# Weight splitting moved within the scalar engine's tile order, output units interleaved, squares summed by VectorE

## Chip, core and metric

The kernel is one launch on one core of a Trainium2 chip. The metric is device time in microseconds (us) of that core; lower is better. Engines: TensorE (PE, with its weight load PEld), VectorE (DVE), ScalarE (ACT), GpSimd (POOL), and SyncE (SP), which issues most of the DMA.

## What is computed

Two identical-shaped decoder layers over 520 tokens (512 new prompt positions and 8 sampled tokens), width 1024, everything in float32. Cut to what matters here, with `rms` an RMS norm with a gain:

```python
x = x + 0.5 * swiglu(rms(x, n_ffn1), w_ffn1_gate, w_ffn1_up, w_ffn1_down)    # hidden 2816
mix, v, new_buf, hT = hybrid_mix(rms(x, n_mix), ...)       # ends in concat(y_a, y_b) @ w_out
x = x + mix
x = x + 0.5 * swiglu(rms(x, n_ffn2), w_ffn2_gate, w_ffn2_up, w_ffn2_down)
gate = sigmoid(rms(x, n_ple) @ w_ple_gate)
x = x + gate * (p @ w_ple_proj)
```

`swiglu(x, wg, wu, wd) = (silu(x @ wg) * (x @ wu)) @ wd`. After the second layer comes a final RMS norm. `hybrid_mix` is a gated spatial mixer beside a linear recurrence; it matters here through its last product, `w_out`.

## The kernel before

**Layout.** x lies in SBUF as 8 tiles of 128 features by 520 tokens (`x[:, o, :]`). Each float32 operand of a product is split into a rounded high part and a remainder (`w_hi`, `w_lo`, `part_hi`, `part_lo`), and a product is the sum of three matmuls (hi·hi, hi·lo, lo·hi). A norm is not applied to x: its gain is put in when x is split, and the row factor `rstd_b` multiplies results. The weights are one stream of 512 KB units, loaded by SP into four `raw` buffers in turn; the load of unit n waits until the semaphore `wlo` says that unit n-4 has been used up. ACT makes the high part (`hi`), DVE the low part (`lo`).

**The feed-forward with seven products.** Three of the four feed-forwards (all but the first) go through `seven_ffn`: gate and up weights of one hidden tile (128 features), each cut in two halves along the 1024 inputs, against x cut in two feature halves and two token halves (A1, A2), are a 2 by 2 block product done with seven products `P1` to `P7` in place of eight, Strassen-Winograd fashion. Each product is twelve matmuls of 260 columns. It wants sums: of weight halves (`tau1` to `tau4`, DVE) and of x blocks (`sigma`, DVE: four operations for each k of 4, from x[k] and x[k+4]; `sigma_hi` on ACT and `sigma_lo` on DVE split them). A feed-forward has 22 hidden tiles in chunks of 8, 8 and 6; after each chunk come 8 down units (`down_part`).

**The order of work** is written out by hand for every engine, with semaphores. For tile t (g stands for the tile of a loop step) PE runs `P1(g+1) P7(g) P2(g+1) P4(g) P6(g+1) P5(g+1) P3(g)`. P1 and P2 read the gate weights themselves, split in slot t % 2 (`gate_cut`): ACT writes `w_hi` (L1024) and the negated weights into `w_lo` (L1025), then POOL adds the weights to that `w_lo` by an accumulating DMA from DRAM (`gate_low`, L539), which leaves the remainder. P6 and P5 read the split of tau1 and tau2: `hi12` on ACT (L1031), `lo12` on DVE (L1489). P7 and P4 read that of tau3 and tau4: `hi34` (L1036), `lo34` (L1494). P3 reads one half of the up weights, `hi_b` (L1041) and `lo_b` (L1499). P4(g) may start only when DVE has read P7's result out of the same PSUM bank (`c22`, L1544: it adds the copy `p5` that ACT made of P5 at L1111). ACT's row for the gate weights is `gate(t)`, called for tile g+3 in loop step g, ahead of `copy_p5(g+1)` and `hi12` of tile g+2.

**Entry into such a feed-forward.** Before it stand 8 units that finish x, one feature tile each: the output projection (L1842 adds to x), or in layer 0's last stage the PLE gate units (L1884). Behind each, ACT (`seven_prep`) copies x times gain to `part_hi` (L1004), keeps x21g (L1009) and squares x into `rs` (L1012); DVE makes `part_lo` (L1431) and, for units 4 to 7, the block sums (`sigma`, L1440 to L1448); POOL adds up the squares (L424, L427). `seven_ahead` prepares the weights of the first tiles. PE then runs `P1(0) P1(1) P2(0)`, `stat1` (the sum of squares over partitions), `P2(1) P6(0) P5(0) P7(0) P4(0)`; ACT takes the root of `stat1`'s result and DVE its reciprocal (`rstd`, L1382).

Of the kernel before, what the change touches and what calls it, by code (L numbers as in the profile page):

```python
# [77 lines left out]

Y_ORDER = (MT, MT + 1, 0, MT + 2, 1, MT + 3, 2, 3)
# [68 lines left out]
def trunk(nc, weights, x_in, p_in, vecs_in, ln_in, bs_in, ws_in, bd_in, sc_in, sh_in,  # L148
          y_out, st_out, v_out):
    ctx = ExitStack()  # L150
    with ctx:
# [94 lines left out]
        gate_neg = sem("gate_neg")  # L246
        gate_lo = [sem(f"gate_lo{b}") for b in range(2)]
# [217 lines left out]
        def _(pool):  # L465
# [89 lines left out]
            for l in range(DEPTH):  # L555
# [17 lines left out]
                sums_and_gates(4 * l + 2, l, 1)  # L573
                sums(4 * l + 3)
                if l + 1 < DEPTH:
                    sums_and_gates(4 * l + 4, l + 1, 0)
                else:
                    sums(4 * l + 4)
# [7 lines left out]
        def _(pe):  # L586
# [49 lines left out]
            def seven_ffn(l, which, u0, g0):  # L636
# [24 lines left out]
                for c, tiles in enumerate(FFN_CHUNKS):  # L661
                    first = c == 0

                    def P1(t):
                        if t < 2:
                            pe.wait_ge(evac, G - 1 + t)
                        else:
                            pe.wait_ge(c21_ev, S + t - 1)
                        pe.wait_ge(gate_lo[gate_slot(t)], 16 * ((S + t) // 2 + 1))
                        kw = (lambda k: pe.wait_ge(xlo, XT * stat + k + 1)) if first and t == 0 else None  # L670
                        product(X(G, t), *gate_w(t, 0), *a11, True, False, kw).then_inc(prod, 1)

                    def P2(t):
                        kw = (lambda k: pe.wait_ge(xlo, XT * stat + KH + k + 1)) if first and t == 0 else None
# [67 lines left out]
                    pe.wait_ge(dlo_s, 2 * (3 * (S // HT0) + c) + 1)  # L742
# [1280 lines left out]
```

## Time and profile before

| | |
|---|---|
| median of 3 runs | 1999.06 us (1995.28 to 2002.83) |
| the profiled execution's own time | 2009.22 us |
| its span, first to last instruction | 2007.4 us |
| PE busy | 1906.4 us, 95% |
| DVE / ACT / POOL busy | 1315.3 / 894.1 / 197.0 us |
| granted TensorE clock, mean | 0.984 of full |

A profile is one execution. PE is busy nearly all the time, so the time is what PE's matmuls take plus the stretches in which PE stands, plus what matmuls lose while the granted clock is low. In a timeline row, the brackets say how long the engine was idle before and who ended that.

### The profile page before, as it was taken

Reading aid. Unit: us, or ns where it says so; the run is one execution under the profiler, and the core shown is the slowest. Engines: PE = TensorE matmul, PEld = TensorE weight load, DVE = VectorE, ACT = ScalarE, POOL = GpSimd, SP = SyncE. Lnnn points to the kernel's source line nnn. Section 1 sums busy time; section 2 is a strip of 40 time slices with the busy share of each in tenths; the row PEclk is TensorE's granted clock in tenths of the full one; section 3 lists DMA queues with packets and bytes.
Section 4 is the critical chain, followed back from the end, with each engine's and each line's share of the span. In section 5 each row is a group of like instructions: output and inputs, shape, how many; then the busy total and the mean of one; then the engine's idle time right before and its main releaser. Section 6 shows DMA issues by size and latency. Waiting matters only on the chain.

```text
span 2007.4 us, 37482 instructions
## 1 busy us (share of the span) xinstructions
PE 1906.4 (95%) x15280; PEld 1872.2 (93%) x15280; DVE 1315.3 (66%) x1889; ACT 894.1 (45%) x1271; POOL 197.0 (10%) x247
## 2 busy tenths in 40 slices
PE   8999999999989999999889999999998999999997
PEld 7999999999989989999888989999998999999996
DVE  6444434578687577577877567577777775766775
ACT  5222312454455354354555354344544553534443
POOL 1000000130100000001200000013202000000012
PEclk9999999999989999999989999999999999999998
DMA  5232222322345354454245354462223444544431
GB/s 203 86 103 85 93 87 93 114 76 75 95 116 143 106 127 141 102 144 134 74 106 134 111 126 145 99 175 97 74 96 95 121 142 100 132 127 115 137 125 47
DMA packets 63690, 225.83 MB, mean 112 GB/s; under 512 B 7152, under 2 KB 9488, under 8 KB 63552
## 3 DMA queue, kind: packets, MB, share of 16 engines
q1 hardware_dynamic: 52576, 184.87, 27.5%
q0 software_dynamic: 10976, 38.98, 10.9%
q8 instruction: 103, 1.69, 0.3%
q14 instruction: 35, 0.29, 0.0%
HBM read 221.52 MB, written 2.31 MB: 111 GB/s over the span
## 4 chain that ended last, share of the span: by engine, by line
PE 65%; DVE 12%; DMA 9%; ACT 8%; issue 5%; POOL 0%; DVEq 0%; SPq 0%; ACTq 0%; POOLq 0%
PE main L596 32%; PE main L736 10%; PE main L632 9%; DMA raw<-weights_dram 8%; PE aux L632 4%; PE aux L736 4%; PE aux L888 2%; ACT w_hi L1031 2%; DVE w_lo L1370 2%; ACT w_lo L1025 2%; ACT w_hi L984 1%; ACT wx L1041 1%; DVE x L1622 1%; DVE tau L1478 1%; DVE tmp L1544 1%
## 5 line engine op out<-in xcount | busy, mean ns | idle before, releaser
L596 PE MATMUL main<-part_hi,w_hi 128*128 128x260 f32 x1888 | 382.4, 284 | 3.4 <-DVE tmp L1643 1.5
L596 PE MATMUL main<-part_hi,w_lo 128*128 128x260 f32 x1888 | 380.1, 283 | 0.0
L596 PE MATMUL main<-part_lo,w_hi 128*128 128x260 f32 x1888 | 379.3, 282 | 0.0
L1370 DVE TENSOR_TENSOR w_lo<-raw,w_hi 128x1024 fp32r<-128x1024 f32 (+1 forms) x194 | 245.8, 1269 | 86.5 <-ACT w_hi L984 82.6
L984 ACT ACTIVATE w_hi<-raw 128x1024 fp32r<-128x1024 f32 (+1 forms) x212 | 218.0, 1033 | 187.2 <-PE main L736 84.7
L632 PE MATMUL main<-part_hi,w_hi 128*128 128x260 f32 x792 | 235.9, 298 | 65.8 <-DVE tmp L1544 44.1
L596 PEld LDWEIGHTS main<-part_hi,w_hi 128*128 128x128 f32 x1888 | 291.6, 188 | 5.8 <-issue 3.4
L596 PEld LDWEIGHTS main<-part_hi,w_lo 128*128 128x128 f32 x1888 | 290.6, 188 | 0.0
L596 PEld LDWEIGHTS main<-part_lo,w_hi 128*128 128x128 f32 x1888 | 290.0, 188 | 0.0
L632 PE MATMUL main<-part_lo,w_hi 128*128 128x260 f32 x792 | 228.9, 289 | 0.0
L632 PE MATMUL main<-part_hi,w_lo 128*128 128x260 f32 x792 | 228.6, 289 | 0.0
L632 PEld LDWEIGHTS main<-part_hi,w_hi 128*128 128x128 f32 x792 | 153.4, 194 | 78.6 <-DVE tmp L1544 55.1
L632 PE MATMUL main<-sig,w_hi 128*128 128x260 f32 x1056 | 200.6, 287 | 0.0
L736 PE MATMUL main<-part_hi,w_hi 128*128 128x260 f32 x816 | 164.6, 283 | 3.0 <-DVE x L1622 3.0
L632 PEld LDWEIGHTS main<-sig,w_hi 128*128 128x128 f32 x1056 | 166.8, 193 | 0.0
L736 PE MATMUL main<-part_hi,w_lo 128*128 128x260 f32 x816 | 164.5, 283 | 0.0
L736 PE MATMUL main<-part_lo,w_hi 128*128 128x260 f32 x816 | 163.9, 282 | 0.0
L632 PEld LDWEIGHTS main<-part_lo,w_hi 128*128 128x128 f32 x792 | 154.5, 195 | 0.1
L632 PEld LDWEIGHTS main<-part_hi,w_lo 128*128 128x128 f32 x792 | 154.4, 195 | 0.0
L632 PE MATMUL main<-sig,w_lo 128*128 128x260 f32 x528 | 151.3, 287 | 0.0
L1036 ACT ACTIVATE w_hi<-tau 128x1024 fp32r<-128x1024 f32 x66 | 70.1, 1062 | 179.3 <-DVE tau L1484 157.0
L539 POOL DMA_DIRECT2D w_lo<-weights_dram x66 | 57.3, 869 | 899.5 <-ACT w_lo L1025 899.1
(253 smaller groups left out, 3665.0 us busy)
## 6 DMA issues: line engine op xcount, KB each, us to landing
raw<-weights_dram SPq DMA_DIRECT2D x344, 512.0 KB, 3.4
w_lo<-weights_dram POOLq DMA_DIRECT2D x66, 512.0 KB, 5.4
x<-x_in_dram SPq DMA_DIRECT2D x4, 520.0 KB, 7.1
y_out<-x SPq DMA_DIRECT2D x8, 260.0 KB, 2.7
mix<-p_in_dram POOLq DMA_DIRECT2D x2, 520.0 KB, 3.8
tau<-ln_dram POOLq DMA_DIRECT2D x2, 512.0 KB, 4.0
tau<-ws_dram POOLq DMA_DIRECT2D x2, 512.0 KB, 4.7
bs<-bs_dram POOLq DMA_DIRECT2D x2, 256.0 KB, 4.1
```

The costliest lines, as they stand in the source:

```text
L539: pool.dma_start(w_lo[:, gate_slot(t), :], weights[n, :, :], accum_op=ALU.add).then_inc(gate_lo[gate_slot(t)], 16)
L596: last = pe.matmul(ps[:, q, 0:HALF], ww[:, s, w], xx[:, k, q * HALF:(q + 1) * HALF], start=(a == 0 and b == 0), stop=(a == kts - 1 and b = ...
L632: last = pe.matmul(ps, ww[:, w], xx(k), start=(start and k == 0 and b == 0), stop=(stop and k == KH - 1 and b == 2), skip_group_check=True)
L736: last = pe.matmul(ps[:, q, 0:HALF], ww[:, j % SLOTS, w], xx[:, k, q * HALF:(q + 1) * HALF], start=(k == 0 and b == 0), stop=(k == tiles - ...
L888: last = pe.matmul(vbank[t] if t < NCH else vs, xx[:, k, c:c + P], ww[:, (U_V + u) % SLOTS, kk * WA:(kk + 1) * WA], start=(k == 0 and b == ...
L984: act.activation(w_hi[:, s, 0:c], raw[:, s, 0:c], ACT.Copy).then_inc(whi, 1)
L1025: act.activation(w_lo[:, gate_slot(t), :], raw[:, n % SLOTS, :], ACT.Copy, scale=-1.0).then_inc(gate_neg, 1)
L1031: act.activation(w_hi[:, 3, :], tau12, ACT.Copy).then_inc(whi, 2)
L1036: act.activation(w_hi[:, 2, :], tau34, ACT.Copy).then_inc(hi34_s, 1)
L1041: act.activation(wx_hi, raw_up(n, 1), ACT.Copy).then_inc(hib_s, 1)
L1370: dve.tensor_tensor(w_lo[:, s, 0:c], raw[:, s, 0:c], w_hi[:, s, 0:c], ALU.subtract).then_inc(wlo, 1)
L1478: dve.tensor_tensor(tau[:, 2 * HB:3 * HB], raw_up(n, 0), raw_up(n, 1), ALU.add)
```

## The change

- `gate_cut` writes `w_lo` first, then `w_hi`, with a semaphore of its own (`gate_hi`); P1 waits for both. In the tile loop ACT calls `gate(g + 2)` behind `hi_b(g)`, in place of `gate(g + 3)` behind `copy_u2(g + 1)`; the low part of down unit 1 is made by DVE in the last tile (`lo(d + 1, 1)`), not ahead of it.
- `ORDER` = (0, 4, 1, 5, 2, 6, 3, 7): output projection and PLE gate units come in this order (the weight stream too), so that x[k] and x[k+4] are finished one behind the other, and the block sums are made at every second unit, not at each of the last four. The regions for the split block sums (`SIG_HI`, `SIG_LO`) are placed anew, and the split of p moves from unit 2 to units 0 and 1.
- For the norms ahead of the seven-product feed-forwards DVE adds the squares (`add_square(dve, ...)`); POOL keeps the accumulating DMAs, and the sums of the other norms.
- `rstd` at the entry is moved ahead of `lo_b(0)`.

```diff
+ORDER = tuple(k for h in range(XT // 2) for k in (h, h + XT // 2))
...
-            def sums_and_gates(stat, l, which):
-
-                for o in range(1, XT):
-                    add_square(pool, stat, o)
-                    if o == XT - 3:
-                        gate_low(l, which, 0)
-                    if o == XT - 2:
-                        gate_low(l, which, 1)
-                for t in range(2, HT0):
+            def gates(l, which):
+
+                for t in range(HT0):
                     gate_low(l, which, t)
...
+                        pe.wait_ge(gate_hi, S + t + 1)
                         pe.wait_ge(gate_lo[gate_slot(t)], 16 * ((S + t) // 2 + 1))
-                        kw = (lambda k: pe.wait_ge(xlo, XT * stat + k + 1)) if first and t == 0 else None
+                        kw = (lambda k: pe.wait_ge(xlo, XT * stat + 2 * k + 1)) if first and t == 0 else None
...
             def gate_cut(n, t, T_):
 
                 act.wait_ge(raw_in[n % SLOTS], 16 * (n // SLOTS + 1))
-                act.activation(w_hi[:, gate_slot(t), :], raw[:, n % SLOTS, :], ACT.Copy)
                 act.activation(w_lo[:, gate_slot(t), :], raw[:, n % SLOTS, :], ACT.Copy,
                                scale=-1.0).then_inc(gate_neg, 1)
+                act.activation(w_hi[:, gate_slot(t), :], raw[:, n % SLOTS, :], ACT.Copy).then_inc(gate_hi, 1)
...
                     copy_u2(1)
-                    gate(3)
                     copy_p5(1)
                     hi12(n + 4, S + 2)
                     for g in range(1, tiles - 1):
                         act.wait_ge(unit, n + 2 * g)
                         hi_b(n + 2 * g, S + g)
+                        gate(g + 2)
                         copy_p1(g + 1)
                         h_hi(g - 1)
                         done(g, "P4")
                         hi34(n + 2 * g + 2, S + g + 1)
                         silu(g)
                         copy_u2(g + 1)
-                        gate(g + 3)
                         copy_p5(g + 1)
...
                     h_hi(t - 1)
+                    gate(t + 2)
                     silu(t)
...
-                    if KH <= o < XT - 1:
-                        sigma_hi(4 * l + 2, o - KH)
+                    if o % 2 and o < XT - 1:
+                        sigma_hi(4 * l + 2, o // 2)
...
                     lo12(n, S)
                     if first:
+                        add_square(dve, stat, XT - 1)
                         sigma_lo(stat, KH - 1)
+                        rstd(stat)
                     lo_b(n, S)
                     tau1(n + 2, S + 1)
                     tau2(n + 2, S + 1)
                     c11(0)
-                    if first:
-                        rstd(stat)
                     c11_r(0)
...
                             down_lo(0)
-                            down_lo(1)
                     t = tiles - 1
                     c12(t - 1)
-                    lo_b(n + 2 * t, S + t, 3)
+                    lo_b(n + 2 * t, S + t, 2)
                     c22(t)
                     hidden(t - 1)
                     h_lo(t - 1)
+                    lo(d + 1, 1)
                     c21(t)
...
+                    x_o = x[:, ORDER[o], :]
+                    dve.tensor_tensor(halves(x_o), pair(main[main_slot(G0 + G_OUT + o)]),
+                                      halves(x_o), ALU.add).then_inc(evac, 1)
+                    if o == 2:
+                        dve.wait_ge(p_v, l + 1)
+                    if o and o % 2 == 0:
+                        sigma_lo(4 * l + 2, o // 2 - 1)
+                    if o >= 2:
+                        add_square(dve, 4 * l + 2, o - 1)
                     seven_x_lo(4 * l + 2, o)
-                    if o >= KH:
-                        sigma(4 * l + 2, o - KH)
+                    if o % 2:
+                        sigma(4 * l + 2, o // 2)
```

How the instructions stand, in three places. First ACT in one step of the tile loop, before (L1024 and L1025 are the gate cut, L1111 `copy_p5`, L1031 `hi12`, L1041 `hi_b`):

```order
L1105 ACTIVATE mix<-main0 128x260
L1024 ACTIVATE w_hi<-raw 128x1024
L1025 ACTIVATE w_lo<-raw 128x1024
L1111 ACTIVATE mix<-aux0 128x260
L1031 ACTIVATE w_hi<-tau 128x1024
L1041 ACTIVATE wx<-raw 128x512
L1099 ACTIVATE mix<-main1 128x260
L1126 ACTIVATE part1_hi<-tmp 128x520
L1036 ACTIVATE w_hi<-tau 128x1024
```

and with the change (L1021 and L1023 are the gate cut, L1108 `copy_p5`, L1028 `hi12`, L1038 `hi_b`):

```order
L1102 ACTIVATE mix<-main0 128x260
L1108 ACTIVATE mix<-aux0 128x260
L1028 ACTIVATE w_hi<-tau 128x1024
L1038 ACTIVATE wx<-raw 128x512
L1021 ACTIVATE w_lo<-raw 128x1024
L1023 ACTIVATE w_hi<-raw 128x1024
L1096 ACTIVATE mix<-main1 128x260
L1123 ACTIVATE part1_hi<-tmp 128x520
L1033 ACTIVATE w_hi<-tau 128x1024
```

The gate cut has gone from ahead of `copy_p5` and `hi12` to behind `hi_b`, and its two copies have changed places.

Second, DVE behind output unit 6 of layer 0, from the addition to x up to the tau sum, before:

```order
L1842 TENSOR_TENSOR x<-main0,x 128x520
L1456 TENSOR_TENSOR sig<-tmp45,sig 128x780
L1458 TENSOR_TENSOR part0_lo<-tmp45,part0_hi 128x260
L1431 SCALAR_TENSOR_TENSOR part0_lo<-x,vecs,part0_hi 128x520
L1440 SCALAR_TENSOR_TENSOR tmp45<-x,vecs,tmp 128x260
L1442 SCALAR_TENSOR_TENSOR tmp45<-x,vecs,tmp 128x260
L1445 SCALAR_TENSOR_TENSOR tmp45<-x,ngain,tmp45 128x260
L1448 SCALAR_TENSOR_TENSOR tmp45<-x,ngain,tmp45 128x260
L1484 TENSOR_TENSOR tau<-tau,raw 128x512
```

and with the change (L429 is the addition of squares):

```order
L1841 TENSOR_TENSOR x<-main0,x 128x520
L1454 TENSOR_TENSOR sig<-tmp45,sig 128x780
L1456 TENSOR_TENSOR part0_lo<-tmp45,part0_hi 128x260
L429 TENSOR_TENSOR rs<-rs 128x520
L1429 SCALAR_TENSOR_TENSOR part0_lo<-x,vecs,part0_hi 128x260
L1482 TENSOR_TENSOR tau<-tau,raw 128x512
L1841 TENSOR_TENSOR x<-main1,x 128x520
L429 TENSOR_TENSOR rs<-rs 128x520
```

Unit 6 has lost its five-operation block (a full-width `part_lo` and four block sums) for one addition of squares and a half-width `part_lo`.

Third, DVE from the last weight split ahead of the feed-forward to the addition `c22` of its first tile, before:

```order
L1494 TENSOR_TENSOR w_lo<-tau,w_hi 128x1024
L1489 TENSOR_TENSOR w_lo<-tau,w_hi 128x1024
L1456 TENSOR_TENSOR sig<-tmp45,sig 128x780
L1458 TENSOR_TENSOR part0_lo<-tmp45,part0_hi 128x260
L1499 TENSOR_TENSOR wx<-raw,wx 128x512
L1466 TENSOR_TENSOR tau<-raw 128x512
L1472 TENSOR_TENSOR tau<-tau,raw 128x512
L1531 TENSOR_TENSOR tmp<-main0,mix 128x260
L1382 RECIPROCAL rstd_b<-rstd_b 128x520
L1535 TENSOR_TENSOR tmp<-tmp,rstd_b 128x260
L1544 TENSOR_TENSOR tmp<-main0,mix 128x260
```

and with the change:

```order
L1492 TENSOR_TENSOR w_lo<-tau,w_hi 128x1024
L1487 TENSOR_TENSOR w_lo<-tau,w_hi 128x1024
L429 TENSOR_TENSOR rs<-rs 128x520
L1454 TENSOR_TENSOR sig<-tmp45,sig 128x780
L1456 TENSOR_TENSOR part0_lo<-tmp45,part0_hi 128x260
L1379 RECIPROCAL rstd_b<-rstd_b 128x520
L1497 TENSOR_TENSOR wx<-raw,wx 128x512
L1464 TENSOR_TENSOR tau<-raw 128x512
L1470 TENSOR_TENSOR tau<-tau,raw 128x512
L1529 TENSOR_TENSOR tmp<-main0,mix 128x260
L1533 TENSOR_TENSOR tmp<-tmp,rstd_b 128x260
L1542 TENSOR_TENSOR tmp<-main0,mix 128x260
```

An addition of squares has come in ahead of the split of the last block sums, and the reciprocal stands ahead of `lo_b`, `tau1`, `tau2` and `c11`, no longer behind them.

## Rows read from the trace of the kernel before

**Rows 1.** First part of the page: busy us (share), instructions of each engine.
```profile
PE 1906.4 (95%) x15280; PEld 1872.2 (93%) x15280; DVE 1315.3 (66%) x1889; ACT 894.1 (45%) x1271; POOL 197.0 (10%) x247
```
**Rows 2.** Waits of PE: engine, line, releaser, us in total, times, longest.
```profile
PE main L632 <- DVE tmp L1544: 44.1, 47, 2.5
PE main L632 <- DMA w_lo<-weights_dram: 15.6, 3, 6.2
```
**Rows 3.** Waits of the other engines.
```profile
ACT w_hi L1024 <- DMA raw<-weights_dram: 93.2, 37, 4.3
...
DVE tau L1466 <- issue: 8.3, 8, 1.9
```
**Rows 4.** Timeline of ACT, DVE, PE, one loop step: start, us, row, [idle before].
```profile
724.70 1.06 ACT L1024 ACTIVATE w_hi<-raw 128x1024 fp32r<-128x1024 f32 x1 [2.62 <-DMA raw<-weights_dram]
...
726.87 1.05 ACT L1031 ACTIVATE w_hi<-tau 128x1024 fp32r<-128x1024 f32 x1
...
723.51 0.69 DVE L1472 TENSOR_TENSOR tau<-tau,raw 128x512 f32<-128x512 f32 x1
...
727.95 1.23 DVE L1489 TENSOR_TENSOR w_lo<-tau,w_hi 128x1024 fp32r<-128x1024 f32 x1 [2.26 <-ACT w_hi L1031]
729.10 0.42 DVE L1544 TENSOR_TENSOR tmp<-main,mix 128x260 f32<-128x260 f32 x1
...
729.57 0.38 PE L632 MATMUL main<-part_hi,w_hi 128*128 128x260 f32 x1 [0.81 <-DVE tmp L1544]
```
**Rows 5.** Timeline of PE, waits ahead of P4: two first tiles, one inner tile.
```profile
571.39 0.39 PE L632 MATMUL main<-part_hi,w_hi 128*128 128x260 f32 x1 [2.04 <-DVE tmp L1544]
...
606.03 0.39 PE L632 MATMUL main<-part_hi,w_hi 128*128 128x260 f32 x1 [2.15 <-DVE tmp L1544]
...
706.86 0.39 PE L632 MATMUL main<-part_hi,w_hi 128*128 128x260 f32 x1 [0.52 <-DVE tmp L1544]
```
**Rows 6.** Stretches of 25 us: length, busy (x) per engine, PEclk, DMA share, GB/s.
```profile
600.00:625.00 25.00, 22.86 (x178) 22.65 (x177) 19.62 (x32) 14.09 (x22) 1.71 (x2) 0.93 0.49 127
...
1050.00:1075.00 25.00, 22.54 (x177) 22.33 (x176) 17.93 (x29) 12.89 (x20) 1.73 (x2) 0.93 0.53 131
...
1725.00:1750.00 25.00, 22.68 (x186) 22.26 (x185) 19.01 (x33) 13.57 (x21) 1.75 (x2) 1.00 0.57 144
```
**Rows 7.** Landing of the accumulating DMAs (line L539), then of the raw loads (L445).
```profile
DMA to landing us min/median/max: 5.1/5.4/7.5
...
DMA to landing us min/median/max: 3.1/3.4/9.5
```
**Rows 8.** Timeline of PE at the three entries: P1 waits, and P4(0) of the third.
```profile
557.33 0.56 PE L632 MATMUL main<-part_hi,w_hi 128*128 128x260 f32 x1 [4.95 <-DMA w_lo<-weights_dram]
...
1000.28 0.56 PE L632 MATMUL main<-part_hi,w_hi 128*128 128x260 f32 x1 [5.17 <-DVE tmp L1387]
...
1553.51 0.56 PE L632 MATMUL main<-part_hi,w_hi 128*128 128x260 f32 x1 [6.15 <-DMA w_lo<-weights_dram]
...
1567.81 0.38 PE L632 MATMUL main<-part_hi,w_hi 128*128 128x260 f32 x1 [2.04 <-DVE tmp L1544]
```
**Rows 9.** Timeline of DVE, ACT and POOL at the first entry.
```profile
542.48 1.57 DVE L1440 SCALAR_TENSOR_TENSOR tmp<-x,vecs,tmp 128x260 f32<-128x260 f32 x1
543.97 0.48 DVE L1442 SCALAR_TENSOR_TENSOR tmp<-x,vecs,tmp 128x260 f32<-128x260 f32 x1
...
547.22 0.69 DVE L1842 TENSOR_TENSOR x<-main,x 128x520 f32<-128x520 f32 x1
...
567.15 3.39 DVE L1382 RECIPROCAL rstd_b<-rstd_b 128x520 f32<-128x520 f32 x1
...
549.51 1.05 ACT L1024 ACTIVATE w_hi<-raw 128x1024 fp32r<-128x1024 f32 x1
...
542.46 1.31 POOL L427 TENSOR_TENSOR rs<-rs 128x520 f32<-128x520 f32 x1 [4.74 <-ACT rs L1012]
...
551.81 0.88 POOL L539 DMA_DIRECT2D w_lo<-weights_dram  x1 [0.80 <-ACT w_lo L1025]
```

More of the change, by code:

```diff
@@ L246, in trunk @@
         gate_neg = sem("gate_neg")
+        gate_hi = sem("gate_hi")
         gate_lo = [sem(f"gate_lo{b}") for b in range(2)]
@@ L572, in _ @@
                 pool.dma_start(praw, p_in[l]).then_inc(p_s, 16)
-                sums_and_gates(4 * l + 2, l, 1)
+                gates(l, 1)
                 sums(4 * l + 3)
                 if l + 1 < DEPTH:
-                    sums_and_gates(4 * l + 4, l + 1, 0)
+                    gates(l + 1, 0)
                 else:
@@ L668, in P1 @@
                             pe.wait_ge(c21_ev, S + t - 1)
+                        pe.wait_ge(gate_hi, S + t + 1)
                         pe.wait_ge(gate_lo[gate_slot(t)], 16 * ((S + t) // 2 + 1))
-                        kw = (lambda k: pe.wait_ge(xlo, XT * stat + k + 1)) if first and t == 0 else None
+                        kw = (lambda k: pe.wait_ge(xlo, XT * stat + 2 * k + 1)) if first and t == 0 else None
                         product(X(G, t), *gate_w(t, 0), *a11, True, False, kw).then_inc(prod, 1)
                     def P2(t):
-                        kw = (lambda k: pe.wait_ge(xlo, XT * stat + KH + k + 1)) if first and t == 0 else None
+                        kw = (lambda k: pe.wait_ge(xlo, XT * stat + 2 * k + 2)) if first and t == 0 else None
                         product(Y(G, t), *gate_w(t, 1), *a12, True, True, kw).then_inc(prod, 1)
@@ L984, in hi, with prep @@
                 act.activation(w_hi[:, s, 0:c], raw[:, s, 0:c], ACT.Copy).then_inc(whi, 1)
-            def prep(stat, o):
-                n = stat * XT + o
+            def prep(stat, o, j=None):
+                j = o if j is None else j
+                n = stat * XT + j
                 if 0 < stat < 4 * DEPTH:
@@ L1307, in _ @@
                     seven_prep(4 * l + 2, o)
-                    if o == 2:
+                    if o == 0:
                         act.wait_ge(p_s, 16 * (l + 1))
@@ L1482, in tau4 @@
                 dve.wait_ge(t12, 2 * T_ + 2)
-                dve.wait_ge(gate_neg, T_ + 1)
+                dve.wait_ge(gate_hi, T_ + 1)
                 dve.tensor_tensor(tau[:, 3 * HB:4 * HB], tau[:, HB:2 * HB], raw_gate(n, 1), ALU.add).then_inc(wlo, 1)
@@ L1841, in _ @@
                     dve.wait_ge(unit, N + U_OUT + o + 1)
-                    dve.tensor_tensor(halves(x[:, o, :]), pair(main[main_slot(G0 + G_OUT + o)]),
-                                      halves(x[:, o, :]), ALU.add).then_inc(evac, 1)
-                    if o > KH:
-                        sigma_lo(4 * l + 2, o - KH - 1)
+                    x_o = x[:, ORDER[o], :]
[3 more added lines that the diff above has]
+                        dve.wait_ge(p_v, l + 1)
+                    if o and o % 2 == 0:
+                        sigma_lo(4 * l + 2, o // 2 - 1)
+                    if o >= 2:
+                        add_square(dve, 4 * l + 2, o - 1)
                     seven_x_lo(4 * l + 2, o)
-                    if o >= KH:
-                        sigma(4 * l + 2, o - KH)
-                    if o == 2:
+                    if o % 2:
+                        sigma(4 * l + 2, o // 2)
+                    if o == 1:
                         dve.wait_ge(p_a, l + 1)
@@ L1874, in _ @@
                         seven_x_lo(4 * l + 4, o - 1)
-                        if o > KH:
-                            sigma(4 * l + 4, o - 1 - KH)
+                        if o % 2 == 0:
+                            sigma(4 * l + 4, o // 2 - 1)
+                        if o >= 2:
+                            add_square(dve, 4 * l + 4, o - 1)
                     if o < (XT - 3 if l + 1 < DEPTH else XT - 1):
@@ L1881, in _ @@
                     dve.wait_ge(f_s, l * FS + HT0 + FS_MIX + HT0 + o + 1)
-                    dve.tensor_tensor(T(2), T(1), proj[:, o, :], ALU.mult).then_inc(x_tmp, 1)
+                    dve.tensor_tensor(T(2), T(1), proj[:, ORDER[o], :], ALU.mult).then_inc(x_tmp, 1)
                     dve.wait_ge(x_tmp, l * XT + o + 1)
-                    dve.tensor_tensor(x[:, o, :], x[:, o, :], T(2), ALU.add).then_inc(x_new, 1)
-                    if o > KH and l + 1 < DEPTH:
-                        sigma_lo(4 * l + 4, o - 1 - KH)
+                    dve.tensor_tensor(x[:, ORDER[o], :], x[:, ORDER[o], :], T(2), ALU.add).then_inc(x_new, 1)
+                    if o and o % 2 == 0 and l + 1 < DEPTH:
+                        sigma_lo(4 * l + 4, o // 2 - 1)
                 if l + 1 < DEPTH:
```

43 lines of the change are left out of this document (21 added, 22 removed).

## Prediction

> **What bounds the kernel now.** I read the page's busy shares first: PE is busy 95% of the span [rows 1], so matmuls set the time and only two things can be won: time in which PE stands, and time lost to a low clock. The change takes no matmul away. Then the waits of PE [rows 2]: 44.1 us in 47 waits end with DVE's `c22` (L1544), 15.6 us in 3 waits with an accumulating DMA into `w_lo`. Where the 47 stand is seen in the timeline of PE [rows 5, 8]: three are P4 of the very first tile of a seven-product feed-forward, 2.04 us each (571.39 and 1567.81 are two of them); six are P4 of the first tile of a later chunk, 0.52 us each (706.86 is one; there P4 follows P7 directly, so it must wait for `c22`, 0.42 us long). The other 38, 44.1 - 6.1 - 3.1 = **34.9 us**, are inner tiles, where P2 stands between P7 and P4 to cover `c22`, and yet PE waits 0.2 to 2.5 us.
>
> Why `c22` is late is read from one loop step of three engines [rows 4]. tau2 is done at 724.2, so `hi12` could be split. But ACT stands 2.62 us for a raw gate tile it needs only two tiles later, cuts it (two copies, some 1.9 us), copies p5, and starts `hi12` at 726.87. DVE, in its own fixed order, stands 2.26 us for it, does `lo12` (1.23) and then `c22` at 729.10; PE starts P4 at 729.57, 0.81 late. The wait of the whole kernel behind this is ACT's 93.2 us at L1024 for raw loads, 37 times [rows 3].
>
> **The change, part by part.** The sum is made against the profiled execution's 2009.2 us, which is 10 us above the median of 1999.06; gains are taken off the median unchanged.
>
> *1. Gate cut behind `hi_b`.* Let T be the end of P3 in the step shown: P4 at 729.57 less 0.81 less three products of twelve matmuls (1.43 us each) gives T = 724.5. With the change `hi12` waits for tau2 and p5 alone: start about 724.3, end 725.3 = T+0.9. DVE does `c12` and `hidden` until T+1.2, `lo12` until T+2.4, and is free before P7 ends at T+2.9; `c22` ends at T+3.4, P2 at T+4.3. The wait is gone with 0.9 us to spare. That margin covers the steps in which tau1 itself is late for its raw load, 8 times and at most 1.9 us [rows 3]: `hi12` moves by that, up to 1 us past the margin in the one worst. I take 2 us as what is left in 38 tiles: **33 us** gained, bounds 17 (half the waits stay) and 34.9.
>
> What is moved past what: the cut is now one tile ahead in place of two. It begins at T+1.4 behind `hi12` and `hi_b`, the `w_lo` copy ends T+2.4, POOL issues 0.3 later (at 551.81, where two copies begun at 549.51 end near 551.5 [rows 9]), and the DMA lands 5.4 us on [rows 7], at T+8.1. (The steps of T are the lengths in [rows 4], with 0.3 to 0.7 us for the short operations.) P1 of that tile stands at T+10.0 (seven products). So 1.9 us of slack; the slowest landing, 7.5 us [rows 7], comes at T+10.2. The second copy (`w_hi`, the new `gate_hi`) ends at T+3.4 and holds nobody: `tau4` of that tile comes a step later. The raw tile was asked for at `tau4` of the step before, T-4.9, and is there at T-1.5 by the median of 3.4 us [rows 7]. `copy_p1` goes back by 2 us to T+3.7, and P6 wants it at T+5.7. I cost all this at nothing; if the cover goes, it is P1 that waits.
>
> The Trainium skill (DMA: Bandwidth & Descriptors, "Anatomy of one DMA — SWDGE (gpsimd) path") gives a fit of 2.0 us plus bytes over 436 GB/s, which by the page would be an estimated 3.2 us for 512 KB. The row says 5.4 for this accumulating kind, and I use the row; by the page the slack would be 2 us more and each entry about 1 to 2 us quicker.
>
> *2. The clock.* A stretch with a wait of 2.15 us (606.03) shows 0.93 granted, so does the one with the longest inner wait; a stretch in which inner waits were at most 1.5 us shows 1.00 [rows 5, 6]. Between the two levels, 1.2 and 2.4 GHz, 0.93 over 25 us costs 25 x 0.07 = 1.75 us of full-clock work. Two such stretches, part of it lying in the wait itself: **3 us** (0 to 3.5).
>
> *3. The entries* (output projection into feed-forward, both layers; PLE gates into feed-forward, once). Let U be the end of the last unit: 557.33 - 4.95 - 1.43 = 550.95. Today the addition of unit 6 waits for DVE, busy with block sums, until 547.22, and ACT starts the second gate cut at 549.51; POOL issues at 551.81, and P1(1) starts at U+6.4, P4(0) at U+20.4 (571.39) [rows 5, 8, 9]. Two things in the rows slow DVE: the block sums of four units in a row, and POOL's additions of squares: the block-sum operation beside POOL's 542.46 row takes 1.57 us, its neighbour 0.48. With the change neither is there. DVE adds unit 6 at U-5.65, ACT begins the cut some 1.7 us later, the `w_lo` copy ends at U-2.9, issue U-2.6, landing **U+2.8**: P1(1) starts there, 3.6 us earlier. Now a new wait: `stat1` needs the sum of squares, whose last addition DVE makes behind `lo12`. P1(1) ends U+4.2, its copy and `hi12` U+5.65, `lo12` U+6.85, the addition (0.7) U+7.5, while PE has ended P2(0) at U+5.65: PE stands 1.9 us where it did not. `stat1` ends U+8.6, the root U+9.3, the reciprocal (3.39 [rows 9]) U+12.7, then `lo_b`, tau1, tau2, `c11` and its scaling (0.35 to 0.7 each) U+15.4, `c22` U+15.9. P4(0) at **U+15.9** where it was U+20.4: 4.5 us. In layer 1 P4(0) stands at 1567.81, with U = 1553.51 - 6.15 - 1.43 = 1545.93: U+21.9, so 6 us. POOL loses seven additions per entry (1.31 us each, off the path), DVE gains them at some 0.7 us each and gives that back by the lost slow operations.
>
> At the PLE entry every unit also costs DVE a scaling, a product and an addition to x. By the lengths above an even unit asks some 7.4 us of DVE and an odd one 4.2, beside 5.75 us of PE: DVE stays late, the second cut's DMA lands within a microsecond of where it does now, and P1(0) (5.17 us idle [rows 8]) moves back by up to 2.4. I take 0, bounds -2 and +2. Entries in all **10 us** (4 to 13).
>
> *4. Chunk ends.* `lo` of down unit 1 now stands in the last tile ahead of `c21`. ACT's silu of that tile ends some 0.1 us later than today; nine chunks: **-0.5 us** (-3 to 0). Interleaving, moved `sig` regions and the earlier split of p add no operation and are ahead of their readers: 0.
>
> Sum: 33 + 3 + 10 - 0.5 = 45.5, so the profiled execution would come at 1963.7 and the median at about **1953 us**.
>
> **Rivals.** *A, the wait stays in part.* `hi12` is freed from the gate cut, but DVE has only some 1.5 us idle per tile of 10; a raw load or `tau2` may be late each time once the step is 0.9 us shorter (tau1 waits already 8 times [rows 3]). Then half the inner waits stay: 17 + 1.5 + 5 = 23 us gained, 1976. *B, no change:* inner tiles are then held by tau1 in nearly every step and the entries lose at `stat1` what they win at P1(1): within 10 us of 1999. Against it: at 723.51 tau2 was in time and the waiting was all ACT's. *C, slower.* The accumulating DMA, with one tile of lead in place of two, is late for P1 in the 39 inner tiles that take their cut in the loop. It decides from a landing 1.9 us above the median; to eat the gain and 10 us more it must wait (45 + 10) / 39 = 1.4 us in each, a landing of 8.7 us where the slowest of 66 took 7.5 [rows 7]. That gives 2009. *D, everything comes:* no inner wait left, the clock at 1.00 through the entries too (their stretches lose several us more), 55 us: 1944.
>
> **Chances.** Forecast with its own spread (1946 to 1962) 0.60, D 0.14, A 0.18, B 0.04, C 0.04. The range takes in A and D: 1942 to 1976. About 0.5% (10 us) is what a measurement of this kernel can tell from no change. Faster by more than that: the forecast, A and D, 0.92; same 0.04; slower 0.04.
>
> **What would show it.** Step 1: PE's waits on `c22` fall from 44.1 us to about 10 (three first tiles of about 1.6, six of 0.52, a rest), ACT's 93.2 us wait for raw loads at the gate cut nearly vanishes, and new PE waits on the DMA at P1 of inner tiles stay few. Step 3: P1(1) about 2.8 us behind the last unit in the two output-projection entries, a new wait of about 2 us ahead of `stat1` that ends with DVE's addition of squares, block sums without a 1.5 us member. Wrong would be: `lo12` still waiting 2 us for `hi12`, PE waiting at P1 for the DMA in every tile, or a PLE entry longer by more than 2 us.

## The result, and the profile after

| | before | after |
|---|---|---|
| median | 1998.24 us (5 runs, 1995.28 to 2002.83) | 2010.78 us (5 runs, 2008.12 to 2012.90) |
| the profiled execution's own time | 2009.22 us | 2011.01 us |
| its span | 2007.4 us | 2009.2 us |
| granted clock, mean | 0.984 | 0.989 |

The ratio is 1.0061 (95% interval 1.0043 to 1.0078): 12.5 us **slower**, where 46 us faster was forecast. The two profiled executions differ by 1.8 us only, since that of before lay 11 us above its median. What they show is where time was won and where the same amount was lost.

First part of the page of after, its row of POOL's DMA queue (packets, MB, share of 16 DMA engines' time), and its rows of the two kinds of weight DMA (size, median us from issue to landing):

```profile
PE 1898.5 (94%) x15280; PEld 1865.3 (93%) x15280; DVE 1314.6 (65%) x1910; ACT 900.0 (45%) x1271; POOL 167.7 (8%) x226
...
q0 software_dynamic: 10976, 38.98, 10.8%
...
raw<-weights_dram SPq DMA_DIRECT2D x344, 512.0 KB, 3.3
w_lo<-weights_dram POOLq DMA_DIRECT2D x66, 512.0 KB, 6.5
```

The same 15280 matmuls took 7.9 us less than in [rows 1], at a granted clock of 0.989 for 0.984, but PE stands 2009.2 - 1898.5 = 110.7 us where it stood 101.0. The accumulating DMA lands after 6.5 us by the median; it was 5.4 [rows 7]. Waits of after, engine, line and releaser, us in total, times, longest:

```profile
PE main L628 <- DMA w_lo<-weights_dram: 60.7, 34, 6.6
...
PE main L628 <- DVE tmp L1542: 9.2, 11, 1.7
...
PE aux L617 <- DVE rs L429: 3.3, 3, 1.3
...
DVE tau L1464 <- issue: 110.9, 39, 4.5
```

Against [rows 2, 3]: the waits on `c22` are down from 44.1 us to 9.2, as forecast. In their place PE waits 34 times for the accumulating DMA, and four of these are at the entries (2.92, 6.56, 2.32 and 3.92 us), so 60.7 - 15.7 = 45.0 us in 30 waits stand at P1 of inner tiles. ACT's 93.2 us for raw tiles at the gate cut are gone, but DVE now stands 110.9 us ahead of tau1 (L1464). "Issue" names no releaser; tau1 reads the raw tile, and the times below show that it starts as the load lands.

One loop step of after, the step of [rows 4], and PE's waits at P1 in it and in the next (start, us, row, idle before; the first row is `lo12`):

```profile
725.63 1.22 DVE L1487 TENSOR_TENSOR w_lo<-tau,w_hi 128x1024 fp32r<-128x1024 f32 x1
...
727.37 0.87 POOL L541 DMA_DIRECT2D w_lo<-weights_dram  x1 [10.86 <-ACT w_lo L1021]
...
727.97 1.54 SPq L447 DMA_DIRECT2D raw<-weights_dram  x2
...
735.16 0.69 DVE L1464 TENSOR_TENSOR tau<-raw 128x512 f32<-128x512 f32 x1 [3.40 <-issue]
...
736.67 1.06 ACT L1028 ACTIVATE w_hi<-tau 128x1024 fp32r<-128x1024 f32 x1 [4.40 <-DVE tau L1470]
...
735.02 0.36 PE L628 MATMUL main<-part_hi,w_hi 128*128 128x260 f32 x1 [1.74 <-DMA w_lo<-weights_dram]
...
747.84 0.36 PE L628 MATMUL main<-part_hi,w_hi 128*128 128x260 f32 x1 [2.42 <-DMA w_lo<-weights_dram]
```

Landing times of what was issued from 724 to 736 us in after: the accumulating DMA, then the raw loads (smallest, median, largest):

```profile
DMA to landing us min/median/max: 7.5/7.5/7.5
...
DMA to landing us min/median/max: 6.9/7.0/7.1
```

The same in before, with its two issues:

```profile
727.00 0.87 POOL L539 DMA_DIRECT2D w_lo<-weights_dram  x1 [10.35 <-ACT w_lo L1025]
...
730.29 1.54 SPq L445 DMA_DIRECT2D raw<-weights_dram  x2
...
DMA to landing us min/median/max: 5.4/5.4/5.4
...
DMA to landing us min/median/max: 3.3/3.7/4.0
```

This is the core of the case. In before SP issues two raw loads, the first 3.3 us behind POOL's accumulating DMA. In after the first goes out 0.6 us behind it. `lo_b` and tau4 free the raw buffers for these loads, and they stand behind `lo12` and `c22` in DVE's order: SP issues 2.34 us behind the start of `lo12` in both kernels (727.95 [rows 4] to 730.29, and 725.63 to 727.97). POOL issued 0.95 us ahead of that start and now issues 1.74 us behind it, since the gate cut went from ahead of `hi12` to behind `hi_b` and took the DMA along. The three transfers of 512 KB then take 6.9 to 7.5 us. The accumulating DMA lands at 727.37 + 7.5 = 734.9, and P1 starts at 735.02, 1.74 us late. A raw load lands near 735.1, and tau1 starts at 735.16, 3.40 us late. `hi12` waits for tau2, which stands behind tau1, and `hi_b` and the next gate cut stand behind `hi12` on ACT, so the next DMA goes out late too and P1 is late again, by 2.42 us.

The first entry of after: POOL, PE at P1(1), ACT's copy of P1(1), DVE's last addition of squares, `stat1`, the reciprocal, P4(0):

```profile
548.39 0.86 POOL L541 DMA_DIRECT2D w_lo<-weights_dram  x1 [4.29 <-ACT w_lo L1021]
...
555.26 0.36 PE L628 MATMUL main<-part_hi,w_hi 128*128 128x260 f32 x1 [2.92 <-DMA w_lo<-weights_dram]
...
557.84 0.39 ACT L1096 ACTIVATE mix<-main 128x260 f32<-128x260 f32 x1 [4.25 <-PE main L628]
...
560.35 0.69 DVE L429 TENSOR_TENSOR rs<-rs 128x520 f32<-128x520 f32 x1
...
561.10 1.14 PE L617 MATMUL aux<-rs,ones 128*128 128x260 f32 x4 [1.20 <-DVE rs L429]
...
563.01 3.41 DVE L1379 RECIPROCAL rstd_b<-rstd_b 128x520 f32<-128x520 f32 x1 [0.74 <-ACT rstd_b L1063]
...
569.67 0.39 PE L628 MATMUL main<-part_hi,w_hi 128*128 128x260 f32 x1 [1.65 <-DVE tmp L1542]
```

and a stretch of 4 us in it (length, busy (x) of PE, PEld, DVE, ACT, POOL, granted clock, DMA share, GB/s):

```profile
554.00:558.00 4.00, 2.74 (x14) 2.77 (x15) 2.01 (x3) 0.16 (x1) 0.00 (x0) 0.72 0.17 50
```

With U = 555.26 - 2.92 - 1.43 = 550.91, POOL issues at U-2.5 as forecast, but the landing takes 6.7 us, P1(1) starts at U+4.35 and P4(0) at U+18.8 (before U+20.4, forecast U+15.9).

### The profile page after: what moved, and what is told of

Its sections match the earlier page's. It is cut to its first block, busy times and chain, and to the rows that moved or that the text cites. A ratio compares the mean times of both kernels' runs of the same rounds, so it can differ in the third digit from the quotient of the medians.

```text
span 2009.2 us, 37487 instructions
## 1 busy us (share of the span) xinstructions
PE 1898.5 (94%) x15280; PEld 1865.3 (93%) x15280; DVE 1314.6 (65%) x1910; ACT 900.0 (45%) x1271; POOL 167.7 (8%) x226
## 3 DMA queue, kind: packets, MB, share of 16 engines
q0 software_dynamic: 10976, 38.98, 10.8%
## 4 chain that ended last, share of the span: by engine, by line
PE 60%; DVE 11%; DMA 10%; issue 10%; ACT 8%; POOL 0%; SPq 0%; ACTq 0%; DVEq 0%; POOLq 0%
PE main L592 31%; PE main L733 10%; PE main L628 7%; DMA raw<-weights_dram 6%; DMA w_lo<-weights_dram 4%; PE aux L733 3%; PE aux L883 2%; PE aux L628 2%; DVE w_lo L1367 2%; ACT w_lo L1021 2%; ACT w_hi L979 2%; DVE tau L1470 1%; DVE tau L1464 1%; ACT wx L1038 1%; DVE x L1620 1%
## 5 line engine op out<-in xcount | busy, mean ns | idle before, releaser
L1367 DVE TENSOR_TENSOR w_lo<-raw,w_hi 128x1024 fp32r<-128x1024 f32 (+1 forms) x203 | 255.7, 1261 | 91.8 <-ACT w_hi L979 88.0
L628 PE MATMUL main<-part_hi,w_hi 128*128 128x260 f32 x792 | 234.3, 296 | 70.6 <-DMA w_lo<-weights_dram 60.7
L1028 ACT ACTIVATE w_hi<-tau 128x1024 fp32r<-128x1024 f32 x66 | 70.0, 1060 | 174.2 <-DVE tau L1470 158.5
```

Of the source, the lines that this page charges most:

```text
L628: last = pe.matmul(ps, ww[:, w], xx(k), start=(start and k == 0 and b == 0), stop=(stop and k == KH - 1 and b == 2), skip_group_check=True)
L1028: act.activation(w_hi[:, 3, :], tau12, ACT.Copy).then_inc(whi, 2)
L1367: dve.tensor_tensor(w_lo[:, s, 0:c], raw[:, s, 0:c], w_hi[:, s, 0:c], ALU.subtract).then_inc(wlo, 1)
```

## The experiments

The comparison of each is with the kernel before on the same chip, whose median there was 2007.72 us for e1 to e4, 1999.34 us for after_again and e5 to e7, and 2010.05 us for e8 and e5_again. So ratios are to be compared, not times across chips.

### e1_gate_back: everything but the move of the gate cut

```diff
                     copy_u2(1)
+                    gate(3)
                     copy_p5(1)
...
                         hi_b(n + 2 * g, S + g)
-                        gate(g + 2)
...
                         copy_u2(g + 1)
+                        gate(g + 3)
...
                     h_hi(t - 1)
-                    gate(t + 2)
```

> The changed kernel with the gate cut called where it was before (gate(3) and gate(g+3) behind copy_u2); entries, unit order, squares on VectorE, w_lo-first and the last tile's order as changed. Theory 'collision' (with the gate cut out of the way of hi12, VectorE frees the raw tiles some 3 us earlier, so that two 512 KB raw loads start within 1 us of the 512 KB accumulating DMA; all three slow down, and P1 and tau1 wait for them): the inner tiles are as before (P4 waits near 35 us, accumulating DMA landing about 5.4 us, no P1 waits in inner tiles), and only the entries are won, 0 to 5 us: about 1995 us. Rival 'the entries and the order of units cost the time': this kernel stays near 2010 us.

Measured: 1997.40 us, ratio **0.9948** (0.9933 to 0.9962).

```profile
PE main L628 <- DVE tmp L1542: 41.3, 50, 1.6
...
PE main L628 <- DMA w_lo<-weights_dram: 15.8, 4, 6.6
```

With the gate cut back in its place, `c22` is late again, P1 of inner tiles never is, and the rest of the change is worth 10.3 us, entries and chunk ends together. The profiled executions (2007.4 and 1993.9 us of span) lie 13.5 us apart: 4.0 us are less standing and 9.5 us less busy matmul time, at a granted clock of 0.992 for 0.984. The long stretch at the lower clock level around the PLE entry is in both (0.80 is granted from 985 to 1020 us in each). What e1 lacks are short ones behind the P4 waits of first tiles and behind the longest waits of inner tiles, as from 565 to 615 us. The row of e1 (columns as above), then that of before:

```profile
565.00:615.00 50.00, 45.34 (x368) 44.30 (x367) 39.66 (x63) 29.58 (x45) 4.29 (x5) 1.00 0.56 134
```

```profile
565.00:615.00 50.00, 45.68 (x351) 45.05 (x349) 39.19 (x60) 28.55 (x43) 3.75 (x5) 0.93 0.51 127
```

The timed runs lie closer together than the two profiled ones: the granted clock was 0.985 to 0.988 in the nine of before on this chip and 0.988 to 0.992 in the five of e1, means 0.003 apart. At 9.5 us for 0.008 this is an estimated 4 us of the 10.3.

### e2_gate_only: the move of the gate cut alone

To the kernel before, only the move of `gate`, and with it the place of the low part of down unit 1; the cut still writes `w_hi` first.

```diff
-                    gate(3)
                     copy_p5(1)
...
                         hi_b(n + 2 * g, S + g)
+                        gate(g + 2)
...
                         copy_u2(g + 1)
-                        gate(g + 3)
...
                     h_hi(t - 1)
+                    gate(t + 2)
```

> The kernel before with only the gate cut moved behind hi_b (and the last tile's order that belongs to it, copies still w_hi first). 'Collision': inner tiles as in the changed kernel or worse (w_lo, and so the DMA, is ready 1 us later): PE waits for the accumulating DMA 50 to 80 us, time 2010 to 2025 us. Rival 'entries cost it': about 1955 to 1965 us.

Measured: 2038.98 us, ratio **1.0153** (1.0136 to 1.0171). Waits, and landing of all 66 accumulating DMAs:

```profile
PE main L632 <- DMA w_lo<-weights_dram: 67.8, 24, 6.2
...
PE main L632 <- DVE tmp L1542: 10.6, 10, 2.5
...
DMA to landing us min/median/max: 5.1/5.9/10.2
```

So the loss is all in the move: 31 us slower alone, though it takes away the waits on `c22` too, and 14 us more than the expectation's upper end. Eight of its inner waits at P1 are of 3.9 to 4.9 us, and the granted clock fell with them: 0.971 to 0.976 in its four runs, where before had 0.985 to 0.988. Here `w_hi` is written ahead of `w_lo`, which puts POOL's issue one copy (about 1 us) later; the change writes `w_lo` first and loses less. That this order makes the difference was not run by itself.

### e3_small_acc and e4_before_small_acc: an eighth of the transfer

The accumulating DMA moves 128 of the 1024 columns. In the other 896 the addition is left out and `w_lo` keeps the negated weights; the instructions stay the same. e3 is the change so altered, e4 the kernel before.

```diff
-                pool.dma_start(w_lo[:, gate_slot(t), :], weights[n, :, :],
+                pool.dma_start(w_lo[:, gate_slot(t), 0:P], weights[n, :, 0:P],
```

> The changed kernel with the accumulating DMA cut to 128 of its 1024 columns (most of the gate weights' low part is left as the negated weights, so the product is another one; nothing else differs). 'Collision': the raw loads land in 3 to 4 us again, tau1 and P1 wait no more in inner tiles, and the time is what was predicted, 1950 to 1960 us. Rival 'chain' (the inner tiles are bound by the fixed order of ACT and VectorE, whatever the DMA): P1 no longer waits but PE stands elsewhere, 1985 to 2010 us.

> The kernel before with the same small accumulating DMA. If the waits for c22 before were, as predicted, due to ACT standing for the raw gate tile ahead of hi12, they shrink only by what that raw load lands sooner (median 3.4 to about 3.1 us): 1985 to 1998 us. If they came from the accumulating DMA slowing the raw loads, they go: below 1975 us.

Measured: e3 1943.98 us, ratio **0.9682** (0.9667 to 0.9697); e4 1995.11 us, ratio 0.9937 (0.9921 to 0.9952). Waits of e3:

```profile
DVE tau L1464 <- issue: 0.8, 1, 0.8
...
PE main L628 <- DMA w_lo<-weights_dram: 6.8, 3, 4.0
...
PE main L628 <- DVE tmp L1542: 5.8, 9, 1.7
```

and of e4:

```profile
ACT w_hi L1024 <- DMA raw<-weights_dram: 92.1, 39, 3.9
...
PE main L632 <- DVE tmp L1544: 42.1, 48, 2.5
```

With a small transfer the change is 51 us faster than the kernel before altered in the same way, P1 waits in no inner tile and tau1 once, for 0.8 us. The time is 6 us below the range expected for it. What the mechanism of step 1 was to bring comes once the transfer is out of the way. e4 shows too that the `c22` waits of before did not depend on the size of the transfer (42.1 us for 44.1).

### after_again: the change a second time

> The changed kernel once more, beside the others on this chip: 1.00 to 1.01 of the kernel before, inner tiles with P1 waits of 1 to 2.5 us and accumulating DMAs landing in 5 to 8 us.

Measured: 2008.85 us, ratio 1.0053 (1.0036 to 1.0070), with 30 waits of PE on the accumulating DMA (47.6 us), 27 of them at P1 of inner tiles, and 39 of tau1 (103.7 us). The result holds on a second chip.

### e6_plain_copy: the same bytes without the addition

POOL's DMA copies the weights over `w_lo` in place of adding them to it, so the remainder of the gate weights is left out; size, queue and issuing engine are the same.

```diff
-                pool.dma_start(w_lo[:, gate_slot(t), :], weights[n, :, :],
-                               accum_op=ALU.add).then_inc(gate_lo[gate_slot(t)], 16)
+                pool.dma_start(w_lo[:, gate_slot(t), :], weights[n, :, :]).then_inc(gate_lo[gate_slot(t)], 16)
```

> The changed kernel with the DMA on GpSimd's queue a plain copy of the same 512 KB in place of an accumulating one (w_lo then holds the weights, so the product is another one). If only the bytes beside the raw loads count, it lands in 4 to 5 us and still collides: 1960 to 2000 us. If the accumulating kind is what slows the others (it reads and writes the SBUF), the raw loads land in 3 to 4 us and the time is 1945 to 1955 us.

Measured: 1944.14 us, ratio **0.9725** (0.9709 to 0.9741). Share of 16 DMA engines taken by POOL's queue (packets, MB, share), landing of its 66 DMAs, and two waits:

```profile
q0 software_dynamic: 10976, 38.98, 6.4%
...
DMA to landing us min/median/max: 3.4/3.6/4.6
...
DVE tau L1463 <- issue: 25.0, 34, 1.6
...
PE main L627 <- DMA w_lo<-weights_dram: 6.9, 2, 4.8
```

In after that queue moves the same 38.98 MB with a share of 10.8%. It isn't the bytes, then, but the accumulating kind: 1.7 times the engine time, and a landing of 5.4 us in before where a copy takes 3.6. It holds at the same distance too: 18 of e6's copies had both loads behind them, the first within 0.6 to 1.0 us, and they still landed after 3.5 to 4.0 us. The raw loads slow down beside the copy as well, against what was expected of them, but less (4.4 to 5.7 us from 724 to 736 us); tau1 waits 25.0 us in place of 110.9, and P1 of no inner tile is late. The Trainium skill (Collectives: The Full Stack, "The bandwidth ceiling: the fold count and why AG ≠ RS ≠ AR") says of ReduceScatter, a collective whose transfers add, that it isn't slowed by the arithmetic but by the two source reads of the addition, which push twice the read traffic of a copy. The 1.7 in engine time here is for another kind of transfer and somewhat below 2, and no run here separates the reads from the addition.

### e5_early_lo and e5_again: the low copy two tiles ahead, the high copy where the change has it

The two copies of the gate cut are taken apart. The copy that lets POOL issue goes back behind `copy_u2`, for tile g+3; the other one, which no DMA waits for, stays behind `hi_b`.

```diff
                         hi_b(n + 2 * g, S + g)
-                        gate(g + 2)
+                        gate_b(g + 2)
...
                         copy_u2(g + 1)
+                        gate_a(g + 3)
                         copy_p5(g + 1)
...
                     h_hi(t - 1)
-                    gate(t + 2)
```

> The changed kernel with the gate cut in two pieces: the w_lo copy of tile g+3 behind copy_u2(g+1) (where the whole cut stood before), the w_hi copy behind hi_b. 'Collision': the accumulating DMA starts some 2.5 us earlier against the raw loads that lo_b and tau4 release, overlaps them by 1 to 2 us and no longer by 5, while ACT's hi12 is delayed by one copy (0.95 us) in place of two and no raw wait: P1 waits below 10 us, P4 waits 10 to 25 us, 1960 to 1975 us on a chip where before takes 1998 to 2008. 'Lead only' (the DMA is simply issued too late for P1, whatever runs beside it): P1 waits also go, so the DMA's landing tells the two apart: 5.5 us by collision, 6.5 by lead only.

> e5_early_lo a second time, beside the kernel before on another run of the chip. Theory (inner waits gone because the accumulating DMA starts ahead of the raw loads again and P1 has two tiles of lead): ratio to the kernel before 0.978 to 0.984, as the first time (0.981); PE waits on the accumulating DMA only at the three entries. Rival (the first result was one chip's luck with the landing times): ratio above 0.985 and inner waits on the DMA.

Measured: 1959.92 us, ratio **0.9807** (0.9790 to 0.9823), and on another chip 1969.68 us, ratio 0.9814 (0.9800 to 0.9829). It computes what the reference does and is faster than both kernels. e5_again waits more, 16.1 us in 28 waits on `c22` and 15.3 us in 4 on the DMA, all four of these at the entries. Waits and one step of e5_early_lo:

```profile
PE main L628 <- DVE tmp L1564: 9.4, 15, 1.6
PE main L628 <- DMA w_lo<-weights_dram: 8.9, 3, 4.3
...
DVE tau L1486 <- issue: 5.9, 8, 1.0
...
717.01 0.87 POOL L541 DMA_DIRECT2D w_lo<-weights_dram  x1 [9.68 <-ACT w_lo L1028]
...
720.31 1.53 SPq L447 DMA_DIRECT2D raw<-weights_dram  x2
...
717.97 1.23 DVE L1509 TENSOR_TENSOR w_lo<-tau,w_hi 128x1024 fp32r<-128x1024 f32 x1 [1.31 <-ACT w_hi L1038]
```

The raw loads are again 3.3 us behind the accumulating DMA; all 66 land after 5.2 us by the median (5.4 in e5_again), tau1 hardly waits, and the step shown takes 10.0 us (POOL issues at 717.01 and 727.01), which is seven products of 1.43 us; its neighbours take 9.6 to 10.5. `lo12` still waits 1.31 us for `hi12`, behind one copy in place of two, and this is short enough for P2 to cover `c22`. Each half can be read against a neighbour: against e1 (0.9948) one copy is out of `hi12`'s way, and against the change (1.0053 on the same chip) the DMA is issued early.

### e7_lo_behind_hi12: in between

As e5, with the low copy for tile g+3 behind `hi12`, ahead of `hi_b`.

```diff
                         copy_u2(g + 1)
-                        gate_a(g + 3)
                         copy_p5(g + 1)
                         if g + 2 < tiles:
                             hi12(n + 2 * g + 4, S + g + 2)
+                        gate_a(g + 3)
```

> As the kernel with the early w_lo copy, but that copy stands behind hi12 of tile g+2, ahead of hi_b. hi12 is not delayed at all; the DMA starts 0.5 us earlier than in the changed kernel and 1.5 to 2 us later than with the early copy. 'Collision': between the two, P1 waits 10 to 40 us, 1965 to 1995 us.

Measured: 1967.67 us, ratio 0.9839 (0.9823 to 0.9856).

```profile
DVE tau L1486 <- issue: 70.2, 39, 3.2
PE main L628 <- DVE tmp L1564: 17.2, 20, 1.6
...
PE main L628 <- DMA w_lo<-weights_dram: 9.1, 3, 3.9
...
731.92 0.86 POOL L541 DMA_DIRECT2D w_lo<-weights_dram  x1 [10.26 <-ACT w_lo L1028]
...
733.04 1.54 SPq L447 DMA_DIRECT2D raw<-weights_dram  x2
```

Here the raw loads go out 1.1 us behind the DMA. All 66 still land after 5.2 us by the median, but the raw loads of this step take 6.5 and tau1 waits in 39 tiles. P1 of inner tiles, with two tiles of lead, waits for no DMA, where 10 to 40 us were expected. So one part of the loss can be seen by itself: slow raw loads cost 8 us against e5, as much as the waits on `c22` are longer (17.2 us for 9.4). The waits at P1 come on top where the DMA itself lands late and has one tile of lead.

The gap between POOL's issue and SP's next one orders the steps. Counted over the whole traces are the accumulating DMAs that both raw loads of a step followed, 39 in each kernel's tile loop but e2's:

| gap, us | DMAs | accumulating DMA, us | raw loads, us |
|---|---|---|---|
| 3.3 to 4.2 | before, e1, e5: all 39 of each | 5.0 to 6.4, medians 5.2 to 5.4 | 3.1 to 6.0 |
| 1.1 to 1.8 | e7: all 39; after: 9 | 4.9 to 5.5, one of 6.7 | 4.8 to 6.7 |
| 0.6 | after: the other 30 | 6.7 to 8.3, median 7.1 | 6.1 to 7.9 |
| 0.3 to 0.7 | e2: 16 | 6.5 to 9.0, median 7.3 | 4.2 to 8.0 |

This also answers the obvious rival, that one tile of lead is too short by itself. In the 9 steps of after with the wider gap P1 was wanted 6.9 to 7.0 us after POOL's issue and never waited. In the other 30 it was wanted after 5.9 to 6.6 us and waited every time. A landing of 5.4 us, the median of before, would have been in time in all 39.

### e8_square_first: the last addition of squares ahead of lo12

```diff
+                    if first:
+                        add_square(dve, stat, XT - 1)
                     lo12(n, S)
                     if first:
-                        add_square(dve, stat, XT - 1)
                         sigma_lo(stat, KH - 1)
```

> As e5_early_lo (low copy of the gate cut behind copy_u2, high copy behind hi_b), but at the three entries DVE makes the last addition of squares ahead of lo12 of the first tile, not behind it. Theory: PE's wait ahead of stat1 (3.5 us in 3 waits in e5_early_lo, longest 1.7) comes from that place alone; it goes below 1 us in all, P6(0) is not delayed in return, since PE stands there anyway, and the reciprocal comes up to 1.2 us earlier: 1 to 3 us less than e5_early_lo run beside it. Rival: the addition waits for ACT's last square, so lo12 is held and the wait moves from stat1 to P6(0): the same time as e5_early_lo or up to 2 us more.

Measured: 1966.29 us (1965.61 to 1969.56), ratio **0.9792** (0.9778 to 0.9805), beside e5_again's 0.9814 on the same chip. The 2.5 us in 3 waits that e5_again has ahead of `stat1` are gone, and at the first entry P4(0) comes 13.2 us behind the start of P1(1) (below), in e5_again 14.3 (555.56 to 569.84).

```profile
555.60 0.36 PE L628 MATMUL main<-part_hi,w_hi 128*128 128x260 f32 x1 [3.04 <-DMA w_lo<-weights_dram]
568.77 0.38 PE L628 MATMUL main<-part_hi,w_hi 128*128 128x260 f32 x1 [1.84 <-DVE tmp L1564]
```

3.4 us between the medians is what was expected (1 to 3) and a little more; the two intervals overlap, so the wait's place is shown and the size of the gain is not. The ratio is the lowest of the kernels that compute the reference, though not clear of e5's 0.9807.

## Why the prediction was wrong

*The step that failed* is in part 1: "So 1.9 us of slack ... I cost all this at nothing". It was worked out of two landing times [rows 7], 5.4 us for the accumulating DMA and 3.4 for a raw load, both measured while the raw loads went out 3.3 us later. The change itself takes that distance away.

The prediction went through what the moved cut is moved past on ACT and counted POOL's issue at T+2.7 (T is the end of P3), but did not ask what SP issues beside it. Its own steps had most of the answer: `c22` ends at T+3.4, and in the trace of before SP's first load goes out 0.8 us behind the end of `c22` (729.52 to 730.29), so at T+4.2, 1.5 us behind POOL and no longer 3.3. The first loop step of each chunk in after comes near this, with a gap of 1.1 to 1.2 us. Its loads took 5.1 to 6.7 us and tau1 of the next step was late (by 1.97 us ahead of the step shown); from there on `c22` no longer had to wait for P7, and the gap fell to 0.6.

Run by run: with the gap at 0.6 us the accumulating DMA took 6.7 to 8.3 us and the raw loads 6.1 to 7.9 (after); without the addition, or with an eighth of the bytes, the same program gives 0.9725 and 0.9682 (e6, e3); with the DMA early again, 0.981 (e5). The slack of 1.9 us was there in the 9 steps with the wider gap (P1 wanted 6.9 to 7.0 us after the issue, the DMA landed after 5.1 by the median). In the others it was shorter, too: in the step shown P1 was wanted at 735.02 - 1.74 = 733.28, 5.9 us after POOL's issue and not 7.3, since tau1 was already late in the step before it.

*Rival C* named the right place, P1 of the inner tiles, and the right waits: 1.4 us in each of 39 forecast, 1.5 us in each of 30 measured. Its chance of 0.04 came from asking for a landing of 8.7 us "where the slowest of 66 took 7.5"; 6.7 to 8.3 us was enough, with tau1 late. It lacked the second half, the raw loads that slow down with it.

*Step 1's gain* was there as argued. `c22` waits fell to 9.2 us in 11 waits: three first tiles of 1.65, six of 0.52, a rest of 1.1; "about 10" was forecast, with the same parts. ACT's 93.2 us vanished. Where transfers don't collide, the gate cut's move gives 2007.72 x (0.9948 - 0.9682) = 53 us on top of e1. The small transfer brings 12.6 us by itself in the kernel before (e4), which leaves about 41, near the 33 + 3 of steps 1 and 2. The time of rival D, 1944 us, is what e3 and e6 took, with another transfer.

*Step 2, the clock.* 3 us were forecast from two inner stretches at 0.93 granted, with waits of 2.15 and 2.46 us in before. In after two others show 0.93, with waits at P1 of 2.45 us (625 to 650 us) and 2.36, and that from 1725 to 1750 us, with one of 2.14, shows 1.00. The waits moved to P1, and so did the loss.

*Step 3, the entries.* 10 us forecast for three. P4(0) moved from U+20.4 to U+18.8, from U+26.7 to U+26.6 (the PLE entry, 0 forecast) and from U+21.9 to U+20.2: 3.4 us in all. In e1, whose three are U+18.3, U+26.7 and U+20.1, they are 3.9 us of the 10.3; an estimated 4 us more are the clock, which the step did not count, and the rest is not told apart. What the step said of DVE held: in before 12 of the 48 block-sum operations took 1.52 to 1.58 us, each beside an addition of squares on POOL, and now all take 0.48 or 0.49; POOL issued at U-2.5. Two terms were mis-sized. The DMA landed after 6.7 us, with a raw load issued 0.7 us behind it that took 6.3: 1.5 us. And behind the wait of 2.92 us P1(1) ran partly at the lower of the two clock levels (0.72 granted from 554 to 558 us): its result was copied 2.6 us after its start where 1.43 was taken, 1.1 us. Together that is 2.7 of the 2.9 us by which P4(0) missed U+15.9. The new wait ahead of `stat1`, 1.9 us forecast, took 1.20, 1.26 and 0.85.

*Step 4, the chunk ends*, can't be read apart; with step 3 it makes e1's 10.3 us, where 9.5 were forecast. That the two agree is in part luck, since the entries gave 3.9 of the 10 us counted for them.

The fit of the Trainium skill (DMA: Bandwidth & Descriptors, "Anatomy of one DMA — SWDGE (gpsimd) path"), an estimated 3.2 us for 512 KB, is near the plain copy of e6 (3.6 us) and not the accumulating kind (4.9 us at the least). The sum would have been further off with it.

## What to carry to other kernels

When a change moves the instruction that a transfer waits for, place its new issue among those of the other queues: here POOL's DMA moved 2.7 us towards two loads that SP sends behind `lo_b` and tau4. The loads then took twice their time and the DMA 1.4 times its own. A landing time from a trace holds only for the distance between transfers that the trace had; when a lead is shortened, read off who else issues within the next few microseconds, and ask what both cost together. Of a pair of instructions moved for one reason, move only the one that is in the way and costs nothing later: taking the two copies apart turned a loss of 0.5% into a gain of 1.9% on the same chip.

## What the runs showed of the hardware

- An accumulating DMA of 512 KB into SBUF took 5.1 to 5.5 us by the median where the next load was issued 1.1 us behind it or later (single ones up to 7.4), a plain copy of the same size from the same queue 3.6, an accumulating one of 64 KB 2.7. Its queue holds the DMA engines 10.8% of the span against 6.4% with the copy, for the same 38.98 MB.
- Two 512 KB loads issued from 0.6 us behind it on made it take 6.7 to 8.3 us and took 6.1 to 7.9 us themselves, against 3.1 to 4.6 in the same stretch of before and e5, where they went out 3.3 us behind it. A plain copy in its place kept its 3.5 to 4.0 us at such gaps. The mean of 112 GB/s over the span, the same in before and after, says nothing of it.
- The kernel before took 1998, 2008, 1999 and 2010 us on four occasions (three chips at least), with a spread of 4 to 8 us on each: about as much from one occasion to the next as the effect of this change, which shows only beside runs of before on the same chip.
- 12 of DVE's 48 block-sum operations took 1.52 to 1.58 us, each of them while POOL added squares; with the squares added by DVE, 0.69 us each, all 48 took 0.48 or 0.49. The order of the units was changed along with it.
